# Handing x over with its channels on partitions, and loading the first weight tile in halves, in a two-block model kernel on one Trainium2 core

## What is computed

```python
def _rmsnorm(x, g):
    xf = x.astype(jnp.float32)
    inv = lax.rsqrt(jnp.mean(xf * xf, axis=-1, keepdims=True) + RMS_EPS)
    return (xf * inv * g.astype(jnp.float32)).astype(x.dtype)
...
    h = x
    for layer in range(DEPTH):
        u = _rmsnorm(h, norm_mix_g[layer])
        proj = jnp.einsum('bsd,de->bse', u, w_in[layer])
```

## Time and profile before

| | |
|---|---|
| Time, median of 3 runs | 2340.91 us (2340.78 to 2341.13) |
| Profiled execution: first to last instruction (its span) | 2339.0 us |
| PE busy / DVE busy / ACT busy | 99% / 72% / 49% |
| Read from memory | 529.67 MB |
| DMA, mean over the span | 228 GB/s |

### The profile page before, as it was taken

One profiled execution on the slowest core, in us unless ns is written; L12 is line 12 of the kernel. 1 busy time (PEld: TensorE's weight loads), 2 busy tenths in 40 slices (PEclk: granted clock), 3 DMA queues, 4 the chain that ended last, 5 costly groups with the idle time before them and its releaser, 6 DMA issues.

```text
span 2339.0 us, 30916 instructions
## 1 busy us (share of the span) xinstructions
PE 2315.7 (99%) x11982; PEld 1967.1 (84%) x11982; DVE 1684.9 (72%) x2105; ACT 1143.1 (49%) x1420; POOL 0.2 (0%) x4
## 2 busy tenths in 40 slices
PE   8999999999999999999999999999999999999998
PEld 7888888888888888888888888788888888888887
DVE  5545778868868868657667754886788658875786
ACT  5445555445435435747356453765444434443444
POOL 0000000000000000000000000000000000000000
PEclk9999999999999999999999999999999999999999
DMA  8552777877877876667829965084556565555564
GB/s 298 191 195 105 255 260 272 304 284 275 300 285 274 300 284 256 239 178 308 300 76 376 343 213 192 8 328 154 191 189 209 190 208 190 189 195 190 189 185 147
DMA packets 136341, 533.45 MB, mean 228 GB/s; under 512 B 19152, under 2 KB 19536, under 8 KB 122400
## 3 DMA queue, kind: packets, MB, share of 16 engines
q1 hardware_dynamic: 135936, 531.73, 64.8%
q10 hardware_dynamic: 288, 0.11, 0.0%
HBM read 529.67 MB, written 2.11 MB: 227 GB/s over the span
## 4 chain that ended last, share of the span: by engine, by line
PE 94%; DVE 3%; ACT 2%; issue 1%; DMA 0%; DVEq 0%; ACTq 0%
PE PSA L818 23%; PE PSA L657 18%; PE PSA L658 18%; PE PSA L659 18%; PE PSA L814 6%; PE PSA L821 6%; PE PSA L864 1%; ACT whi L1340 0%; DVE u L2177 0%; PE PSA L763 0%; PE PSA L1007 0%; DVE wlo L2021 0%; PE PSA L1023 0%; DVE QZ L2381 0%; PE PSA L1137 0%
## 5 line engine op out<-in xcount | busy, mean ns | idle before, releaser
L2021 DVE TENSOR_TENSOR wlo<-raw,whi 128x1024 fp32r<-128x1024 f32 x788 | 933.0, 1218 | 337.2 <-ACT whi L1340 336.0
L1340 ACT ACTIVATE whi<-raw 128x1024 fp32r<-128x1024 f32 x788 | 799.8, 1052 | 466.9 <-DMA raw<-in_w_down 174.2
L818 PE MATMUL PSA<-u,whi 128*128 128x512 f32 x2368 | 566.1, 391 | 0.0
L818 PEld LDWEIGHTS PSA<-u,whi 128*128 128x128 f32 x2368 | 435.0, 188 | 84.3 <-DVE u L2177 0.2
L657 PE MATMUL PSA<-whi,u 128*128 128x512 f32 x1088 | 426.2, 392 | 3.4 <-DVE wlo L2021 3.4
L659 PE MATMUL PSA<-whi,u 128*128 128x512 f32 x1088 | 423.5, 389 | 0.0
L658 PE MATMUL PSA<-wlo,u 128*128 128x512 f32 x1088 | 423.5, 389 | 0.0
L657 PE MATMUL PSA<-whi,ahi 128*128 128x512 f32 x856 | 333.9, 390 | 0.0
L659 PE MATMUL PSA<-whi,alo 128*128 128x512 f32 x856 | 333.1, 389 | 0.0
L658 PE MATMUL PSA<-wlo,ahi 128*128 128x512 f32 x856 | 333.1, 389 | 0.0
L657 PEld LDWEIGHTS PSA<-whi,u 128*128 128x128 f32 x1088 | 204.2, 188 | 47.5 <-issue 3.0
(11 more groups left out here) (353 smaller groups left out, 1295.1 us busy)
## 6 DMA issues: line engine op xcount, KB each, us to landing
raw<-in_w_up SPq DMA_DIRECT2D x300, 512.0 KB, 3.4
raw<-in_w_in SPq DMA_DIRECT2D x208, 512.0 KB, 3.5
mod_slot<-in_w_mod_rows SPq DMA_DIRECT2D x96, 1024.0 KB, 5.9
raw<-in_w_down SPq DMA_DIRECT2D x192, 512.0 KB, 3.4
raw<-in_w_out SPq DMA_DIRECT2D x64, 512.0 KB, 3.4
raw<-in_w_down2b SPq DMA_DIRECT2D x20, 512.0 KB, 3.7
c_all<-in_c_rows SPq DMA_DIRECT2D x3, 1024.0 KB, 4.7
xc<-in_ctx SPq DMA_DIRECT2D x2, 1024.0 KB, 5.9
```

The source lines that it names most:

```text
L818: mm = pe.matmul(both, wh[:, c], u_pair[:, k, :], start=k == 0, stop=k == KD - 1)
L1340: AF(whi[:, n % SLOTS, 0:w], raw[:, n % SLOTS, 0:w], ACT.Copy).then_inc(hi_done, 1)
L2021: TT(wlo[:, n % SLOTS, 0:w], raw[:, n % SLOTS, 0:w], whi[:, n % SLOTS, 0:w], ALU.subtract).then_inc(lo_done, 1)
```

## The change

The host hands over a second form of x, `xT`, with channels on partitions: for each of the 16 chunks 256 token values and, in a 257th column, the norm's gain. ACT and DVE form `uhi` and `ulo` from it straight from SBUF, and the transposes of x, their identity and `keep_awake` at the start go. x in rows (`h`) is still wanted for the sum of squares and the residual; it is now one 2 MB transfer behind tile 7. The small constants that came ahead on ACT's queue go into SP's later loads, and ACT's queue carries the first two chunks of `xT` instead. Tile 0 is loaded, split and multiplied in two halves; in tiles 0 to 3 PE does the products with `whi` first (`first_tiles`). `mix_squares` moves behind tile 10, `mix_inverse` behind tile 11. The conversion of the mask bytes (`levels`) moves from behind block 1 to the start of block 4. `wake_up` gives PE 13 matmuls on zeros at the start. Other edits renumber waits, since the first eight counts of `tp_ready` are gone and some loads share a semaphore.

The diff, cut to its core:

```diff
--- before.py
+++ after.py
...
+        xT = z_at("xT", [P, KD, TOK + 1], F32, 68 * K)
+        warm = z_at("warm", [P, P], F32, 0)
...
-        ld = {n: sem("ld_" + n) for n in ("ident", "x0", "x1", "x2", "vec", "cb", "lev", "xc", "ws", "wlr", "gf", "bl", "gh", "c", "gs", "gt", "out")}
+        X_PIECES = {"first": (0, 1), "second": (1, 2), "pair1": (2, 4), "pair2": (4, 6), "pairs34": (6, 10), "pairs567": (10, KD)}
+        ld = {n: sem("ld_" + n) for n in ("x", "first_tile", *X_PIECES, "cb", "xc", "wlr", "gf", "gh", "c", "gs", "gt", "out")}
...
-        HOOKS_X = {-1: (0,), 0: (1,), 1: (2, 3), 2: (4, 5), 3: (6, 7)}
-        X_PIECES = (slice(0, 512), slice(512, 1024), slice(1024, D))
+        PAIR_IN = {1: "pair1", 2: "pair2", 3: "pairs34", 4: "pairs34", 5: "pairs567", 6: "pairs567", 7: "pairs567"}
+        HI_FIRST = 4
         LAST_0 = ((0, 1024), (1024, 2048))
         LAST_1 = ((0, 512), (512, 1024), (1024, 1536), (1536, 2048))
         LAST_0_ACT, LAST_1_ACT = (0,), (1,)
-        LOADED = 16 * 5
+        LOADED = 16 * 6
...
-                            if p.name == "in1" and isinstance(i, int) and i == 0 and b == 0 and 1 <= t < len(X_PIECES):
-                                x_piece(t)
+                            if p.name == "in1" and isinstance(i, int) and i == 0 and b == 0:
+                                if 1 <= t <= 4:
+                                    x_piece(("pair1", "pair2", "pairs34", "pairs567")[t - 1])
+                                if t == 0:
+                                    sp.dma_start(raw[:, 0, 0:NBLK], src[:, 0:NBLK]).then_inc(ld["first_tile"], 16)
+                                    sp.dma_start(raw[:, 0, NBLK:], src[:, NBLK:]).then_inc(arrived[0], 16)
+                                    continue
                             tile(src, p, i, p.main_at(b, t))
+                            if p.name == "in1" and isinstance(i, int) and i == 0 and (b, t) == (0, 7):
+                                load(h[:, :, :], t_in["x"].rearrange("(t p) c -> p t c", p=P), "x")
...
-                cols = X_PIECES[n]
-                load(h[:, :, cols], t_in["x"][:, cols].rearrange("(t p) c -> p t c", p=P), f"x{n}")
-
-            x_piece(0)
+                k0, k1 = X_PIECES[n]
+                load(xT[:, k0:k1, :], t_in["xT"][:, k0:k1, :], n)
...
-                    load(ca[:, P:], t_in["const_a"][:, P:], "cb")
-                    load(lev_in[:, :], t_in["levels"], "lev")
+                    load(ca[:, :], t_in["const_a"], "cb")
+                    load(lev_in[:, :], t_in["levels"], "cb")
                     load(bgate[:, :], t_in["b_gate"].partition_broadcast(P), "cb")
                     load(cb[:, :], t_in["const_b"], "cb")
                     load(wf[:, :, :, :], t_in["w_fourier"], "cb")
-                    load(vec[:, NV_FIRST:], t_in["vec"][:, NV_FIRST:], "cb")
...
+
+            def wake_up(times):
+
+                pe.wait_ge(c_done, 1)
+                for _ in range(times):
+                    pe.matmul(PSA[:, 7, 0:P], warm[:, :], warm[:, :], start=True, stop=True)
+
+            def first_tiles(p):
+
+                for t in range(HI_FIRST):
+                    wh, wl = whi[:, t, :], wlo[:, t, :]
+
+                    def product_of(kk, x, w, first, last):
+                        for tt in range(TC):
+                            k = 2 * t + kk
+                            mm = pe.matmul(PSA[:, p.bank(0) + tt, :], x[:, k, tt * P:(tt + 1) * P], w[:, kk * NBLK:(kk + 1) * NBLK], start=first and k == 0, stop=last and k == p.k - 1)
+                        return mm
+
+                    if t == 0:
+                        pe.wait_ge(tp_hi, 1)
+                        product_of(0, uhi, wh, True, False)
+                        pe.wait_ge(tp_val, 1)
+                        product_of(0, ulo, wh, False, False)
+                        product_of(0, uhi, wl, False, False)
+                        pe.wait_ge(hi_done, 1)
+                        product_of(1, uhi, wh, False, False)
+                        pe.wait_ge(u_ready, 1)
+                        product_of(1, ulo, wh, False, False)
+                        pe.wait_ge(lo_done, 1)
+                    else:
+                        pe.wait_ge(hi_done, t + 1)
+                        for kk in range(2):
+                            product_of(kk, uhi, wh, False, False)
+                        pe.wait_ge(u_ready, t + 1)
+                        for kk in range(2):
+                            product_of(kk, ulo, wh, False, False)
+                        pe.wait_ge(lo_done, t + 1)
+                        product_of(0, uhi, wl, False, False)
+                    product_of(1, uhi, wl, False, True).then_inc(tile_used, 1)
...
-                        for t in range(NG if p.name == "out1" and new else 4 if p.name == "up2_0" and new else 0, p.per_block):
+                        if new and p.name == "in1":
+                            first_tiles(p)
+                        for t in range(NG if p.name == "out1" and new else HI_FIRST if p.name == "in1" and new else 4 if p.name == "up2_0" and new else 0, p.per_block):
...
-            pe.wait_ge(ld["ident"], 16)
-            keep_awake(4)
-            transposes(0, (0, 1))
-            keep_awake(5)
-            stream(BY["in1"], u0=0, between={(0, t): lambda t=t: transposes(0, (2 * t + 2, 2 * t + 3)) for t in range(3)})
+            wake_up(13)
+            stream(BY["in1"], u0=0)
...
-                        for n in range(len(X_PIECES)):
-                            act.wait_ge(ld[f"x{n}"], 16)
+                        act.wait_ge(ld["x"], 16)
...
+
+            def x_high(k):
+
+                return AF(uhi[:, k, :], xT[:, k, 0:TOK], ACT.Copy, scale=xT[:, k, TOK:])
+
+            def first_tile():
+
+                for kk, (piece, loaded, done) in enumerate((("first", ld["first_tile"], tp_hi), ("second", arrived[0], hi_done))):
+                    act.wait_ge(ld[piece], 16)
+                    ins = x_high(kk)
+                    if kk:
+                        ins.then_inc(tp_hi, 1)
+                    act.wait_ge(loaded, 16)
+                    c = slice(kk * NBLK, (kk + 1) * NBLK)
+                    AF(whi[:, 0, c], raw[:, 0, c], ACT.Copy).then_inc(done, 1)
+
+            def x_pair_high(n):
+
+                act.wait_ge(ld[PAIR_IN[n]], 16)
+                for k in (2 * n, 2 * n + 1):
+                    ins = x_high(k)
+                ins.then_inc(tp_hi, 1)
...
+                act.wait_ge(ld["cb"], LOADED)
...
-            between = {"in1": {(0, 7): mix_squares}, "dn1_3": ctx_norm, "inC": lat_norm, "dn2_2": {(1, 2): lambda: root_table(2)}}
-            act.dma_start(ca[:, 0:P], t_in["const_a"][:, 0:P]).then_inc(ld["ident"], 16)
-            act.dma_start(vec[:, 0:NV_FIRST], t_in["vec"][:, 0:NV_FIRST]).then_inc(ld["vec"], 16)
+            between = {"in1": {(1, 2): mix_squares}, "dn1_3": ctx_norm, "inC": lat_norm, "dn2_2": {(1, 2): lambda: root_table(2)}}
+            for n in ("first", "second"):
+                k0, k1 = X_PIECES[n]
+                act.dma_start(xT[:, k0:k1, :], t_in["xT"][:, k0:k1, :]).then_inc(ld[n], 16)
...
-                    first = {t: lambda ns=ns: transposes_hi(0, v_("g_mix"), None, ns) for t, ns in HOOKS_X.items()}
+                    first = {-1: first_tile, **{n - 1: lambda n=n: x_pair_high(n) for n in range(1, 8)}}
...
-                stream(p, first, between.get(p.name, {}), early={"out1": 7, "inL": 2, "out2": 8}.get(p.name, 0), rest=rest)
+                stream(p, first, between.get(p.name, {}), early={"in1": 1, "out1": 7, "inL": 2, "out2": 8}.get(p.name, 0), rest=rest)
...
+                                masks_as_bytes()
...
-                turns(dve, p, body, unrolled=p.name in ("in1", "inC", "dn1_3"), after_first=(lambda: gates_end(NARROW[p.name])) if p.name in NARROW else masks_as_bytes if p.name == "in1" else None)
+                turns(dve, p, body, unrolled=p.name in ("in1", "inC", "dn1_3"), after_first=(lambda: gates_end(NARROW[p.name])) if p.name in NARROW else None)
...
-                dve.wait_ge(ld["lev"], 16)
+                dve.wait_ge(ld["cb"], LOADED)
...
+                dve.memset(warm[:, :], 0.0).then_inc(c_done, 1)
...
+
+            def x_low(k):
+
+                return STT(ulo[:, k, :], xT[:, k, 0:TOK], xT[:, k, TOK:], uhi[:, k, :], ALU.mult, ALU.subtract)
+
+            def first_tile():
+
+                dve.wait_ge(tp_hi, 1)
+                x_low(0)
+                TT(wlo[:, 0, 0:NBLK], raw[:, 0, 0:NBLK], whi[:, 0, 0:NBLK], ALU.subtract).then_inc(tp_val, 1)
+                dve.wait_ge(tp_hi, 2)
+                x_low(1).then_inc(u_ready, 1)
+                dve.wait_ge(hi_done, 1)
+                TT(wlo[:, 0, NBLK:], raw[:, 0, NBLK:], whi[:, 0, NBLK:], ALU.subtract).then_inc(lo_done, 1)
+
+            def x_pair_low(n):
+
+                dve.wait_ge(tp_hi, n + 2)
+                for k in (2 * n, 2 * n + 1):
+                    ins = x_low(k)
+                ins.then_inc(u_ready, 1)
...
```

(42 more changed lines are left out.)

8 lines of the change are left out of this document (2 added, 6 removed).

## The result

| | before | changed |
|---|---|---|
| Median of 21 runs | 2341.64 us (2340.35 to 2342.64) | 2344.22 us (2343.03 to 2346.48) |
| Span of the profiled execution | 2339.0 us | 2341.8 us |
| First matmul of tile 12 | 47.11 | 49.89 |
| ACT takes block 1 out of PSUM | 58.31 | 61.23 |

The ratio is 1.0012, 95% interval 1.0007 to 1.0018: 2.6 us slower by the medians, where 3.5 had been forecast (2344.4), and under the 0.2% that was called no change.

What follows compares the result with a forecast made beforehand. PE (99% busy) bounds the kernel, with the DMA queue also full at the start; tile 12 3.1 us later plus 0.4 for the clock gives 3.5 above the 2339.0 span, with 1.9 around it 2344.4 us; range 2339.5 to 2347.

Steps and rivals of the forecast that it cites:

- Gain at the front: Block 0 on PE: would end at about 29 instead of 36.2, a gain of about 7 us.
- ten such: Wake-up matmuls at PE's start: ten were read as taking 1.28 us warm, costing nothing before data comes.
- The queue: DMA queue: 2.1 MB more ahead of tile 10 would make it land at 37.5 instead of 32.4, bounds 36.9 to 38.3.
- The second rival: DMA queue: tile 10 lands about 3 us earlier than forecast, time 2341, change worth nothing; chance 0.12.
- ACT's list: In-order ACT: squares behind tile 10's split make 12.7 us from its landing to tile 12, at 50.2, 3.1 later.
- The clock: PE after its stalls: half clock loses 1.7 us each, mostly hidden; 0.4 us added, bounds 0 and 2.5.
- the signs: Observations to show the forecast right, among them PE idle about 5.5 and 2 to 4 us ahead of tiles 10 and 11.
- The third rival: PE's clock: both long stalls cost it and low clock reaches tile 12, 5.6 us slower, 2346.5; chance 0.17.
- The first rival: Start: tile 10 lands in time, ACT's order rules, tile 12 at 41.0, 6.1 us earlier, 2334.8; chance 0.14.
- The limit from the page: DMA queue: at about 358 GB/s the extra bytes take 5.9 us and the sum ends 0.8 higher; not adopted.

Runs made afterwards that it cites:

- e2: Changed kernel with squares and reciprocal one tile earlier (squares between splits of tiles 9 and 10), transfers unchanged; 2340.92 us, ratio to before 1.0001.
- e1: Changed kernel with the 3 MB of constants issued behind tile 15 instead of tile 9; 2335.12 us, ratio to before 0.9975.
- e3: Kernel before with one more 2 MB load of x, read by nobody, behind tile 7; 2341.56 us, ratio to before 1.0001.
- e4: Kernel before with only the squares moved behind tile 10's split and the reciprocal behind tile 11; 2341.94 us, ratio to before 1.0000.
- e5: Kernel before with both the extra 2 MB load and the squares and reciprocal moved later; 2344.18 us, ratio to before 1.0013.
- e8: Changed kernel with filler matmuls on PE, 34 behind tile 9 and 25 behind tile 10; 2344.16 us, ratio to before 1.0011.
- e11: Changed kernel with constants behind tile 15, 16 fillers at the middle stall, squares, reciprocal and evacuation behind tile 13's split; 2333.26 us, ratio to before 0.9965.
- e10: Changed kernel with constants behind tile 15, squares behind tile 11's split, tile 0 whole, 24 instead of 13 wake-up matmuls; 2336.14 us, ratio to before 0.9977.

## Why the prediction was right

**Gain at the front.** 7 us forecast; tile 4 at 18.00 was 7.25 us earlier than before. The pieces were close: tile 0 done at 9.1 (8.8 said), tile 1 without the wait that I had expected at 9.4, 0.53 us short at tile 4 (half a us said). One row was misread: the rows count each float32 matmul of the program on `warm` or the identity twice (`wake_up(13)` is x26), so the "ten such" in 1.28 us were five. The thirteen took 4.64 us and ended just as tile 0 could start. In e2 they took 5.91 and tile 0 waited for them until 6.62; why they differ is open, and tile 4 came at 18.08 all the same.

**The queue.** The step on which all rested was the landing of tile 10: 32.4 plus the extra bytes at 409 GB/s, 37.5. It was issued at 21.40 and took 15.9 us to land, 37.3. e1 shows that its place behind the constants is the cause, e3 that the bytes by themselves cost nothing as long as PE wants the tile later than it comes. The second rival, a landing some 3 us earlier, is out by the 37.3. Constants moved in the kernel before were not run; there PE has no idle time from tile 4 to block 1 that they could take away. (The queue's 1.25 us for a tile should be 1.28, 512 KB at 400 KB/us, and ACT's splits behind a full queue do start 1.27 to 1.28 us apart; nothing hangs on it.)

**ACT's list.** 12.7 us were summed from landing to tile 12; it took 49.89 - 37.3 = 12.6. e2 shows this part's share with the late transfer, e4 that it costs nothing with an early one. e5 shows that the two together are the change's loss, whatever the front does.

**The clock.** Here the forecast was too high. PE was at half clock after its 5.08 us stall, for the whole of tile 10 (5.1 us for 2.7), more than the 1.7 us that I took from the earlier trace rows. It was hidden, as forecast, and tile 11 then ran at full clock. The idle time ahead of tile 11 was thus 1.09 us, not the 2.2 of the sum (the signs had said 2 to 4), and no half clock followed it. The 0.4 us that I added for it didn't come; e8 shows that the clock had no part in the loss. The third rival is out by that run. Without this term the sum is 3.1, against 2.9 measured at block 1 and 2.6 by the medians.

**The level.** That 2344.4 was forecast and 2344.22 measured is in part luck. The forecast stood on 2340.91, the median of three runs; the 21 runs beside the changed kernel gave 2341.64. The base was 0.7 us too low and the step, 3.5 for 2.6, 0.9 too large, and the two nearly cancel.

**The first rival** (the front gain stays, 2334.8) was not what the change does, but its sum, the one with a free queue, is what e1 measured: tile 12 at 41.0 forecast and 41.04 found, 2335.1 for the median. Its loss of about 1 us to the order on ACT was there to be had: tile 12 starts at 39.53 in e11.

**The limit from the page.** The estimate from the limit of about 358 GB/s in the Trainium skill, "DMA: Bandwidth & Descriptors" (Specifications), put tile 10 at 38.3. It landed at 37.3, with 412 GB/s from 30 to 39 us, so here the measurement decides: the rate of the rows was the right one.

## What to carry to other kernels

An early phase has two budgets, the compute engine's and the transfer queue's. Before shortening the first, look at when each later tile lands and when it is wanted: here 7 us of slack in the queue had hidden 5 MB of x and constants, and a faster front together with 2 MB more used it up. Move what isn't wanted soon behind what is, and never put spare-time work in an in-order list behind a wait for a transfer that may be late. To find which of two costs is at fault, put them into the old kernel one by one and together: here neither cost anything measurable alone. In these runs fillers for the clock paid only where no other wait stood behind the stall: in the changed kernel they gave nothing (e8), ahead of tile 0 they gave 2.3 us (e10).
